# Second router: the first expert's turned rows formed on the matrix engine from a mask of ranks, and the residual placed in two parts

## The reference

```python
def hier_moe(x, w_group, b_group, w_router, b_router, w_gate, w_up, w_down):
    g_logits = (x @ w_group).astype(jnp.float32) + b_group
    g_prob = jax.nn.softmax(g_logits, axis=-1)
    _, g_idx = lax.top_k(g_logits, 1)
    p_group = jnp.take_along_axis(g_prob, g_idx, axis=-1)
    e_all = jnp.einsum('nd,dge->nge', x, w_router).astype(jnp.float32) + b_router
    e_logits = jnp.einsum('ng,nge->ne', jax.nn.one_hot(g_idx[:, 0], MOE_GROUPS, dtype=jnp.float32), e_all)
    e_prob = jax.nn.softmax(e_logits, axis=-1)
    top_p, top_i = lax.top_k(e_prob, MOE_TOP_K)
    weights = p_group * top_p / jnp.sum(top_p, axis=-1, keepdims=True)
    ...
    for e in range(MOE_EXPERTS):
        hdn = jax.nn.silu(x @ w_gate[e]) * (x @ w_up[e])
        y = y + combine[:, e:e + 1] * (hdn @ w_down[e])
    return y
```

## Time and profile before

| | us |
|---|---|
| median of 3 runs | 1146.42 (1146.33 to 1148.82) |
| the profiled execution, its own time | 1145.1 |
| its span, first to last instruction | 1143.0 |
| PE busy | 1014.7 (89%) |
| VectorE (DVE) busy | 367.4 (32%) |
| ACT busy | 197.1 (17%) |
| POOL busy | 77.7 (7%) |
| mean granted TensorE clock | 0.947 |

### The profile page before, as it was taken

One profiled execution on the slowest core, in us unless ns is written; L12 is line 12 of the kernel. 1 busy time (PEld: TensorE's weight loads), 2 busy tenths in 40 slices (PEclk: granted clock), 3 DMA queues, 4 the chain that ended last, 5 costly groups with the idle time before them and its releaser, 6 DMA issues.

```text
span 1143.0 us, 19745 instructions
## 1 busy us (share of the span) xinstructions
PE 1014.7 (89%) x8287; PEld 613.7 (54%) x8287; DVE 367.4 (32%) x760; ACT 197.1 (17%) x372; POOL 77.7 (7%) x126
## 2 busy tenths in 40 slices
PE   3899999999997999999999950996986899998896
PEld 1443433456446888888888740443543555444442
DVE  1101899367436111111111105245516311111112
ACT  2200031344023100000000003213513100000001
POOL 4200000001001100000000002000010100010000
PEclk9899999998995999999999985997999799999998
DMA  9999777650013799999999639231022599999993
GB/s 344 400 387 378 275 268 273 258 231 4 11 65 145 247 373 417 385 385 402 393 393 411 272 132 396 98 147 74 0 76 112 188 409 412 401 396 397 417 427 150
DMA packets 70688, 312.92 MB, mean 274 GB/s; under 512 B 5768, under 2 KB 7496, under 8 KB 60144
## 3 DMA queue, kind: packets, MB, share of 16 engines
q1 hardware_dynamic: 58656, 283.64, 63.8%
q0 software_dynamic: 6448, 15.60, 4.1%
q10 hardware_dynamic: 5536, 12.98, 3.0%
HBM read 301.98 MB, written 14.81 MB: 277 GB/s over the span
## 4 chain that ended last, share of the span: by engine, by line
PE 79%; DMA 11%; DVE 4%; issue 2%; ACT 1%; SPq 1%; POOL 1%; PEldq 0%; ACTq 0%; DVEq 0%
PE ps L481 52%; PE ps L892 10%; DMA ring<-in_moe_w_gate 7%; PE ps L494 3%; PE ps L919 3%; PE ps L805 2%; DMA ring<-in_ada_w 2%; PE ps L881 2%; PE ps L977 2%; DMA ar<-y_rows,sm 1%; SPq L431 1%; PE ps L739 1%; PE ps L905 1%; DMA y_rows<-ar 1%; PE ps L1096 1%
## 5 line engine op out<-in xcount | busy, mean ns | idle before, releaser
L481 PE MATMUL ps<-ring,ar 128*32 128x384 f32 (+5 forms) x3992 | 507.9, 470 | 14.1 <-DMA ring<-in_moe_w_gate 7.0
L481 PEld LDWEIGHTS ps<-ring,ar 128*32 128x32 f32 (+2 forms) x3992 | 218.5, 121 | 148.7 <-issue 81.9
L892 PE MATMUL ps<-ring,ar 128*32 128x128 f32 x1632 | 183.8, 273 | 0.0
L892 PEld LDWEIGHTS ps<-ring,ar 128*32 128x32 f32 x1632 | 176.7, 110 | 0.0
L481 PE MATMUL ps<-hT,ring 128*128 128x512 f32 x256 | 114.2, 601 | 0.1
L481 PE MATMUL ps<-ring,hT 128*128 128x512 f32 x192 | 83.7, 595 | 1.5 <-ACT hT L1195 1.5
L481 PEld LDWEIGHTS ps<-hT,ring 128*128 128x128 f32 x256 | 48.2, 192 | 64.1 <-issue 63.6
L1895 DVE SCALAR_TENSOR_TENSOR ar<-ar,cpar 128x512 f32<-128x512 f32 x120 | 79.6, 740 | 0.0
L1777 DVE COPY ar<-ps 128x384 f32<-128x384 f32 (+1 forms) x32 | 15.7, 491 | 166.8 <-PE ps L908 83.5
L494 PE MATMUL ps<-ring,silu_c 128*32 128x512 f32 x384 | 49.4, 633 | 21.6 <-DMA ring<-in_ada_w 21.6
L481 PEld LDWEIGHTS ps<-ring,hT 128*128 128x128 f32 x192 | 36.1, 190 | 48.5 <-issue 46.9
(11 more groups left out here) (301 smaller groups left out, 840.3 us busy)
## 6 DMA issues: line engine op xcount, KB each, us to landing
ring<-in_moe_w_gate SPq DMA_DIRECT2D x33, 2048.0 KB, 13.2
ring<-in_moe_w_up SPq DMA_DIRECT2D x33, 2048.0 KB, 13.7
ring<-in_moe_w_down SPq DMA_DIRECT2D x33, 2048.0 KB, 14.1
ring<-in_ada_w SPq DMA_DIRECT2D x24, 2048.0 KB, 14.4
ring<-in_even_w_in SPq DMA_DIRECT2D x5, 2048.0 KB, 18.7
ring<-in_odd_w_in SPq DMA_DIRECT2D x3, 2048.0 KB, 15.4
y_rows<-ar ACTq DMA_DIRECT2D x17, 288.0 KB, 7.2
ring<-in_even_w_out SPq DMA_DIRECT2D x2, 2048.0 KB, 11.0
```

The source lines that it names most:

```text
L481: return nc.tensor.matmul(o, l, r, start=start, stop=stop)
L892: m = nc.tensor.matmul(ps[96:128, bank, g * P:(g + 1) * P], xgT[:, p, c, 32 * g:32 * g + 32], w[:, c, 3 * P:HID], start=c == 0 and g == 0, ...
```

## The change

It concerns the second layer alone (l == 1).

- The residual's matmuls for tile 1 are placed ahead of the second tile's turning, those for tile 0 stay behind the rows. For the banks to be free, both tiles are turned in banks 4 and 5 (`turn_bank`), and the second turning waits for the modulated copies of the first.
- As soon as the ranks are there, VectorE forms `place` (rank + 1 where the token is one of expert 0's, else 0) and compares it with `count_row` (1 to 64) to a mask `pick` of 128 x 2 x 64. PE multiplies the rows in SBUF, `h2s`, by the mask (`first_picked`: eight column blocks by two tiles, 16 matmuls of 64 columns): that gives the turned rows of expert 0 in PSUM bank 2, where the turning put them before.
- The first expert's gather and its turning are left out; POOL's and PE's counts are changed accordingly. The products for the indices come behind `first_picked` and go to bank 3.
- `slot_col` is started earlier on VectorE. Three small loads count on an existing semaphore (`small_in`), so that the number of semaphores stays.

```diff
+        pick = hidT[:, 0, 2, :].rearrange("p (j n) -> p j n", j=NLAT)
+        count_row, place = hidT[:, 0, 3, 0:CAP[1]], hidT[:, 1, 3, 0:NLAT]
+        IDX_BANK = (0, 3)
+        def turn_bank(l, j):
+            return 4 + 2 * (j % 2) if l == 0 else 4
@@ rows_turned
-                    if j >= 2:
+                    if l == 1 and j >= 1:
+                        pe.wait_ge(sem("hT_act" if h == 0 else "hT_dve"), q)
+                    elif j >= 2:
                         pe.wait_ge(sem("hT_act" if h == 0 else "hT_dve"), q - 1)
-                        m = nc.tensor.transpose(ps[:, 4 + 2 * (j % 2) + h, cc * P:(cc + 1) * P],
+                        m = nc.tensor.transpose(ps[:, turn_bank(l, j) + h, cc * P:(cc + 1) * P],
@@ rows_and_router
+                def residual_placed(j):
+                    for h in range(2):
+                        nc.tensor.matmul(acc(j, h), ident, x[:, j, h * 512:(h + 1) * 512], start=True, stop=False,
+                                         skip_group_check=True)
+                if l == 1:
+                    pe.wait_ge(sem("x_added"), 2 * NT + 2 * NLAT)
+                    residual_placed(1)
                 rows_turned(l, n - 1)
...
                 if l == 1:
-                    pe.wait_ge(sem("x_added"), 2 * NT + 2 * NLAT)
-                    for j in range(NLAT):
-                        for h in range(2):
-                            nc.tensor.matmul(acc(j, h), ident, x[:, j, h * 512:(h + 1) * 512], start=True, stop=False,
-                                             skip_group_check=True)
+                    residual_placed(0)
...
+                if l == 1:
+                    pe.wait_ge(sem("h2_act"), NT + NLAT)
+                    first_picked()
                 pe.wait_ge(sem("slots_ready"), l + 1)
                 for k in range(2 * n):
-                    m = mm(ps[:, 0, 0:NTL], slot_hot[:, k, :], tile_hot[:, k * NTL:(k + 1) * NTL], k == 0, k == 2 * n - 1)
+                    m = mm(ps[:, IDX_BANK[l], 0:NTL], slot_hot[:, k, :], tile_hot[:, k * NTL:(k + 1) * NTL],
+                           k == 0, k == 2 * n - 1)
@@ new
+            def first_picked():
+                pe.wait_ge(sem("picked"), 1)
+                for c in range(KC):
+                    for j in range(NLAT):
+                        m = mm(ps[:, 2, CAP[1] * c:CAP[1] * (c + 1)], h2s[:, j, c * P:(c + 1) * P], pick[:, j, :],
+                               j == 0, j == NLAT - 1)
+                m.then_inc(sem("xgT_ps"), 1)
@@ experts
-                xt(l, 0, 0)
+                if l == 0:
+                    xt(l, 0, 0)
@@ router (VectorE)
+                if l == 1:
+                    V.tensor_scalar(count_row, ps[:, 1, 384:384 + CAP[1]], 1.0, None, ALU.add)
                 link(V.tensor_reduce(r("gm"), lgv[:, :, 0:4], AX_X, ALU.max))
...
+                if l == 1:
+                    link(V.scalar_tensor_tensor(place, ranks[:, :, 0], 1.0, r16("MM")[:, :, 0], ALU.add, ALU.mult))
+                    V.tensor_tensor(pick, count_row.unsqueeze(1).to_broadcast([P, NLAT, CAP[1]]),
+                                    place.unsqueeze(2).to_broadcast([P, NLAT, CAP[1]]), ALU.is_equal).then_inc(sem("picked"), 1)
...
+                if l == 1:
+                    V.tensor_scalar(slot_col, ps[:, 1, 384:384 + NTL], 64.0, float(NO_TOKEN), ALU.mult, ALU.add)
...
-                    link(V.tensor_scalar(slot_col, ps[:, 1, 384:384 + NTL], 64.0, float(NO_TOKEN), ALU.mult, ALU.add))
                     link(V.tensor_scalar(slot_col, slot_col, slot_of, None, ALU.add))
@@ gathers (POOL)
-                gather(l, 0, 0)
+                if l == 0:
+                    gather(l, 0, 0)
```

More of the change, by code:

```diff
@@ L931, in do_down @@
                 return m
+            def first_picked():
[5 more added lines that the diff above has]
+                m.then_inc(sem("xgT_ps"), 1)
             def xt(l, e, p):
-                pe.wait_ge(sem(f"xg_in{p}"), 16 * (8 * l + 1) + 8 * (e - p))
+                pe.wait_ge(sem(f"xg_in{p}"), 16 * (8 * l + 1 - l * (1 - p)) + 8 * (e - p))
                 if not (isinstance(e, int) and e == 0 and l == 0):
@@ L1215, in tail_norm @@
                     if j:
-                        modulated(l, 1, j - 1, 4 + 2 * ((j - 1) % 2))
-                modulated(l, 1, n - 1, 4 + 2 * ((n - 1) % 2))
+                        modulated(l, 1, j - 1, turn_bank(l, j - 1))
+                modulated(l, 1, n - 1, turn_bank(l, n - 1))
             def rows(l):
@@ L1583, in tail_norm @@
                 if j:
-                    modulated(l, 1, j - 1, 5 + 2 * ((j - 1) % 2))
+                    modulated(l, 1, j - 1, turn_bank(l, j - 1) + 1)
                 dve.wait_ge(sem("sq_done"), SQBASE[k] + j + 1)
@@ L1618, in router @@
                 V.tensor_copy(logitsT[:, 0:(n - 1) * P], ps[:, 0, 0:(n - 1) * P]).then_inc(sem("logitsT"), 1)
-                modulated(l, 1, n - 1, 5 + 2 * ((n - 1) % 2))
+                modulated(l, 1, n - 1, turn_bank(l, n - 1) + 1)
                 link(V.memset(R["MM"][:, 16 * n:16 * n + 16], 0.0))
@@ L1673, in router @@
                 ct = cmp_t[:, 0:2 * n * MAXOV].rearrange("p (t k) -> p t k", t=2 * n)
-                ranks = ps[:, 1, 256:256 + 16 * n].rearrange("p (j e) -> p j e", e=16).unsqueeze(1).to_broadcast([P, 2, n, 16])
+                ranks = ps[:, 1, 256:256 + 16 * n].rearrange("p (j e) -> p j e", e=16)
+                if l == 1:
+                    link(V.scalar_tensor_tensor(place, ranks[:, :, 0], 1.0, r16("MM")[:, :, 0], ALU.add, ALU.mult))
+                    V.tensor_tensor(pick, count_row.unsqueeze(1).to_broadcast([P, NLAT, CAP[1]]),
+                                    place.unsqueeze(2).to_broadcast([P, NLAT, CAP[1]]), ALU.is_equal).then_inc(sem("picked"), 1)
+                ranks = ranks.unsqueeze(1).to_broadcast([P, 2, n, 16])
                 V.tensor_tensor(r32("t12"), r32("M12"), ranks, ALU.mult)
@@ L1707, in router @@
                                                 ALU.mult, ALU.add))
-                    link(V.tensor_scalar(slot_col, ps[:, 1, 384:384 + NTL], 64.0, float(NO_TOKEN), ALU.mult, ALU.add))
                     link(V.tensor_scalar(slot_col, slot_col, slot_of, None, ALU.add))
                 dve.wait_ge(sem("idx_ps"), l + 1)
-                V.tensor_scalar(idx, ps[:, 0, 0:NTL], float(NO_TOKEN), None, ALU.add).then_inc(sem("idx_ready"), 1)
+                V.tensor_scalar(idx, ps[:, IDX_BANK[l], 0:NTL], float(NO_TOKEN), None, ALU.add).then_inc(sem("idx_ready"), 1)
                 dve.wait_ge(sem("g_exp"), l + 1)
@@ L2030, in odd_mixer @@
             def odd_mixer():
-                dve.wait_ge(sem("norm_g_in"), 48)
+                dve.wait_ge(sem("small_in"), 16 * N_SMALL + 48)
                 dve.wait_ge(sem("k_sq"), 1)
@@ L2136, in gather @@
                     .then_inc(sem("idx_col"), 1)
-                pool.wait_ge(sem("idx_col"), NEXP * l + e + 1)
+                pool.wait_ge(sem("idx_col"), NEXP * l + e + 1 - l)
                 pool.sem_inc(sem("waits_passed"), 1)
@@ L2146, in overflow @@
                 with pool.If(n > 0):
-                    pool.wait_ge(sem("xg_in0"), 8 * NEXP * (l + 1))
+                    pool.wait_ge(sem("xg_in0"), 8 * NEXP * (l + 1) - 16 * l)
                     pool.wait_ge(sem("xgT_ps"), NEXP * (l + 1) - 1)
@@ L2202, in _ @@
                              (gb[:, 3, P:2 * P], A["odd_k_norm_g"].to_broadcast([P, P]))):
-                pool.dma_start(dst, src).then_inc(sem("norm_g_in"), 16)
+                pool.dma_start(dst, src).then_inc(sem("small_in"), 16)
             pool.wait_ge(sem("oh_taken"), HEADS)
```

## The result

| | before | after |
|---|---|---|
| median of 20 runs each, us | 1152.61 (1144.95 to 1157.18) | 1143.47 (1140.36 to 1151.24) |
| ratio, with 95% interval | | 0.9944 (0.9926 to 0.9962) |
| profiled execution: time, span | 1145.1, 1143.0 | 1142.67, 1140.6 |

The change is faster: by 0.56% of 1150, 6.4 us, if one takes the ratio (the means differ by 6.4 too), and by 9.1 if one takes the difference of the medians. The two differ because the times of both kernels are spread over 11 to 12 us, with more of them near either end than between; a median lies in one or the other half by a few runs. The mean of the three ratios is 0.9959, 4.7 us.

The account below looks back on a forecast made before the run. The prediction took the second layer's weight stream, started by the first gate product's end, as the bound. Router savings summed to 9.9 us warm, cut to 4.3 for a clock fall: 1146.42 - 4.3 = 1142.1, range 1135.5 to 1144.0.

Parts of the forecast that it names:

- What bounds the kernel: Second layer's expert stage: a stream of 42 weight blocks, 88 MB at about 405 GB/s, 218 us, started by first gate product's end.
- one-for-one passing on: Weight stream: each microsecond by which the first gate product ends earlier is a microsecond off the total.
- 1): Second layer's router, residual in two parts, bank 4 for both tiles: net 1.0 us earlier, 0.4 later if the clock falls.
- 2): VectorE up to the expert choice: one more operation, 0.1 us; choice known at 878.9, ranks end 2.3 us earlier.
- 3): Behind the choice, a small VectorE operation stays bound to POOL's memset: VectorE goes on 1.3 us earlier, not 2.3.
- 4): VectorE's added place and mask operations behind the ranks: mask ready at 881.3, slots at 884.9.
- 5): PE's 16 added mask matmuls, 32 records: 3.9 us at full clock, 7.7 at half; index products follow, 1.0 us.
- 6): First gather, landing and transposes removed, 6 us; gate product from 886.3, first weight load 9.9 us earlier if warm.
- 7): Expert 1's gathered rows land at 890.6, turned at 894.2: cover 3.6 us, beyond that loss one for one.
- The clock: PE's clock falls to half around the mask products, into the gate product; gain 4.3 us instead of 9.9, chance 0.50.
- warm rival: PE's clock stays full throughout the second layer's router and first gate product: gain 9.9 us, 1136.5; chance 0.36.
- How the numbers follow: Whole kernel: gain 4.3 taken from 1146.42, median of the runs shown, giving 1142.1; chance of faster 0.76.

Follow-up runs that it names:

- e2_split_only: The kernel before with only the residual in two parts and both tiles turned in bank 4; ratio to before 0.9993 (0.9967 to 1.0018).
- f1_before_filler: The kernel before with four unused 512-column matmuls behind the ranks and four behind the index products; one time, 1145.35 us.
- e3: The changed kernel with the residual whole behind the rows and four banks for the turning, as before; ratio to before 0.9933 (0.9904 to 0.9963).
- f3: The changed kernel with POOL's second-layer memset released by the slots instead of the choice; ratio to before 0.9951 (0.9928 to 0.9973).
- a0_after: The changed kernel again, no edit; median 1145.84 us beside 1149.2 for the kernel before, ratio 0.9972 (0.995 to 0.9994).
- e1: The changed kernel with two unused 512-column matmuls between ranks and mask products; median 1137.07 us of 6 runs, ratio to before 0.9907.
- g3: The changed kernel with two unused 512-column matmuls between ranks and mask products, run again; 1137.33 us (6 runs), ratio to before 0.9896.
- g4_after_again: The changed kernel once more, no edit, on the chip of three others; 1147.38 us (12 runs), ratio to before 0.9961 (0.9935 to 0.9987).
- f2_narrow_filler: The changed kernel with seven unused 16-column matmuls between ranks and mask products; one time, 1141.99 us.
- g1: The changed kernel with POOL's memset released by the slots and one unused 512-column matmul before the mask products; ratio to before 0.9901.

## Why the prediction was off in size

**What bounds the kernel: right.** From the first load to the end it is 242.5 to 244.7 us in all profiles, whatever stands before; DMA share 1.00 from 896.6 to 1107.8 in `after`. But the one-for-one passing on had a small leak. The three kernels that gather first (before, e2_split_only, f1_before_filler) have 242.5 to 243.2, those with the mask 242.9 to 244.7, on average a microsecond more, though the two ranges overlap. The prediction priced the two gathers that now fall beside the stream at 1 us; that would fit. No run took them away, so this is argued, not shown.

**1) and 2), residual and choice: right, 0.25 too good.** Second turning 0.5 later behind T (forecast 0.4), 1.13 long (1.05); ranks 2.06 earlier (forecast 2.3). What the sum did not have: without this part T to R is not always 16.95. In e3 and f1 it was 19.7, since a second fall of the clock took the rows. With it, it was 14.76 to 14.90 in ten profiles. So the part also keeps that stretch steady, which the forecast gave no price.

**3), POOL's memset: right, and shown.** 1.46 us beside the memset, 0.17 without; e2 gained 0.92 where 1.3 were forecast, f3 0.9 where 1.1 were. The rule of the Trainium skill that the prediction weighed ("SBUF — State Buffer", Who interferes with whom), an exclusive lock between GpSimd and such VectorE operations, agrees with these runs.

**4) and 5), mask: right.** Mask products 17.4 behind T (forecast 17.0). Where the clock fell, the 40 records took 7.95 to 8.57 (forecast 8.6), where it held, 4.54 to 4.62 (forecast 4.9).

**6), gate product: the term with the widest range.** From its start to the load it took 5.17 in `after`, and 6.5 in `a0_after` (897.86 to 904.38). The forecast took 5.9 (890.0 to 895.9), between 4.0 and 6.5.

**7), expert 1's rows: right.** Nothing waits there; the turning follows the up product at once in all profiles.

**The clock: right.** The forecast said it would fall and took 4.3 for the gain; the three profiles give 5.2, 3.6 and 3.6, mean 4.2, against the one profile of the kernel before. The warm rival's price was 9.9; e1 and g3, where the clock holds, give 10.04. The rival itself, with its chance of 0.36, did not come: none of the three profiles of the changed kernel kept the clock. The place is right, too: at 882 by the forecast, behind 0.9 us of mask products; it was 883.9, 0.6 us into them.

**The step that failed** is the first sentence of "How the numbers follow": the gain was set against 1146.42 as if that were the level of the kernel before. It was the median of three runs, all of which lay in the lower part of what 20 runs then showed, 1144.95 to 1157.18, and nothing in the range provided for it. Against that level 1143.47 is 3.0 us less; against the median of the 20, 1152.61, it is 9.1. Nor is that one the level: beside the later runs the median of the kernel before was 1149.2, 1148.61 and 1150.41. That 1143.47 lies only 1.4 us from the forecast 1142.1 is therefore luck: the level was taken 6.2 us lower than that comparison showed it, and the difference came out 4.8 larger. The term that was mis-sized is a zero: the spread of the kernel before, most of it in all that lies ahead of T. The same code reached T between 864.19 and 872.83 in the 13 profiles. A second part of it lies in the router: the forecast took T to R of the kernel before as fixed at 16.95, and f1 has 19.69 for the same code. Three windows of the kernel before (T 864.33), columns as above:

```profile
30.00:46.00 16.00, 13.04 (x63) 6.21 (x56) 5.40 (x11) 5.04 (x9) 5.95 (x11) 0.82 1.05 390
146.00:152.00 6.00, 6.00 (x21) 2.38 (x23) 6.00 (x11) 0.49 (x1) 0.00 (x0) 1.00 0.91 340
264.50:275.00 10.50, 10.50 (x116) 6.63 (x112) 8.46 (x21) 4.57 (x7) 0.00 (x0) 1.00 0.01 2
```

The same windows of the changed kernel where T was late, `g4_after_again` (T 872.09):

```profile
30.00:46.00 16.00, 12.78 (x55) 6.95 (x48) 5.09 (x11) 3.40 (x8) 3.30 (x6) 0.50 1.05 386
146.00:152.00 6.00, 6.00 (x20) 1.43 (x19) 6.00 (x10) 0.00 (x0) 0.00 (x0) 0.50 0.00 0
264.50:275.00 10.50, 10.50 (x88) 9.97 (x86) 2.96 (x6) 5.81 (x11) 0.00 (x0) 0.50 0.00 0
```

All of this is code that the change leaves alone, though the later windows meet it a few microseconds apart. In all three stretches the clock was at half in the one and not, or only partly, in the other. The seven profiles with T at 868 or later have a mean clock of 0.66 to 0.83 from 142 to 152 us, the six with T under 867 have 1.00. The times agree: of the 29 runs of the kernel before that stand beside a0_after, the fastest (1145.0) had a mean clock of 0.949 and the slowest (1156.76) one of 0.939. So the spread of the whole goes with the granted clock, as the one in the router does, in other places; no run changed those places, so that it is the cause there is argued, not shown. What decides it in one execution or the next stays open; so does whether 6.4 us in the first comparison, against 3.2 and 4.5 in the next two, is more than chance, since the intervals overlap; all three are near the 4.3 of the sum, and an execution of the kernel before with 19.7 from T to R would explain the larger one too.

## What to carry to other kernels

Where narrow matmuls stand between waits, read the granted clock before counting them: here the stretch from the ranks to the first load took 15.8 to 17.4 us without and 11.0 with two wide matmuls of useless work, which was worth more than the finer of the two edits. Before a gain of a few microseconds is set against a level, find out how far that level moves by itself: compare stretches within a profile, from one landmark to the next, and give the total a range that holds the spread of all the rest. Bringing a signal forward also brings forward whatever else it releases; here POOL's memset took back about half of the 2 us that the ranks had gained.

## What the runs showed of the hardware

- The granted clock fell while PE was busy without a gap, on records of 16 to 64 columns (f2_narrow_filler), and held over the same stretch with four records of 512 (e1_filler). The profile's busy time counts both alike. Each of the two is one execution, e1_filler's was repeated in g3_filler_again. A record of 128x128 weights with 16 to 64 columns took 0.11 to 0.12 us at full clock (1.71 for 14 in f2, 4.54 for 40 in g1) and 0.21 to 0.24 at half (8.57 for 40 in g4, 1.91 for 8 in the kernel before).
- A VectorE operation (tensor_scalar) on four columns took 1.46 us beside a GpSimd memset (`after`) and 0.17 without (f3); the tensor_tensor and tensor_reduce operations in front of it ran beside the same memset at their usual 0.22, and the tensor_tensor issued behind it ended with it, after 1.39.
- Code that is the same in all kernels came to the same point, T, at 864 to 873 us; the changed kernel alone at 865.94, 872.13 and 872.09.
